# Gated feed-forward layers: high and low activation parts as one 512-column moving operand, with pairs of PSUM banks

## The reference, cut to what matters

```python
# in the first model, twice:
h = rms_norm(x, norm_ffn[l]) * (1.0 + sc_f) + sh_f
gt, up = jnp.split(h @ w_ffn_in[l], 2, axis=-1)
x = x + g_f * ((jax.nn.silu(gt) * up) @ w_ffn_out[l])
# second model, four times
def swiglu(h, w_gate, w_up, w_down):
    return (jax.nn.silu(h @ w_gate) * (h @ w_up)) @ w_down
x = x + 0.5 * swiglu(rms_norm_2(x, ffn_norm[layer, j]), ...)
```

## Time and profile before

| | |
|---|---|
| Median of 3 runs | 2282.91 us (2274.06 to 2283.78) |
| Profiled execution | 2283.06 us |
| Its span, first to last instruction | 2281.1 us |
| Mean granted TensorE clock | 0.945 of full speed |
| TensorE busy | 2092.5 us |
| VectorE busy | 1469.7 us |
| ScalarE busy | 986.5 us |

### The profile page before, as it was taken

The page is one execution under the profiler, slowest core; times in us unless marked ns, Lnnn a source line. Parts: engine busy times, 40 slices in busy tenths (PEclk is TensorE's granted clock), DMA queues, the critical chain, the costliest instruction groups (busy, mean ns, idle before and its releaser), DMA issues. The chain is left out here.

```text
span 2281.1 us, 36778 instructions
## 1 busy us (share of the span) xinstructions
PE 2092.5 (92%) x15344; PEld 1975.8 (87%) x15344; DVE 1469.7 (64%) x2515; ACT 986.5 (43%) x1486; POOL 27.5 (1%) x47
## 2 busy tenths in 40 slices
PE   3799979998799889999999888899999998789999
PEld 3678879997679879999998668799999998688999
DVE  6568667775577466547766557467657747755773
ACT  2355533333345533334335545443344335654342
POOL 0101000000001000000000000000000000000000
PEclk7789999999889989999999898999999999799999
DMA  8335537884435347555555323345555553222554
GB/s 284 128 123 187 201 103 249 272 272 141 149 134 199 112 129 231 182 179 185 184 178 193 112 74 104 119 138 182 179 186 182 181 174 114 92 93 93 185 181 134
DMA packets 266084, 372.70 MB, mean 163 GB/s; under 512 B 8384, under 2 KB 160192, under 8 KB 265920
## 3 DMA queue, kind: packets, MB, share of 16 engines
q1 hardware_dynamic: 264224, 367.48, 49.5%
q10 hardware_dynamic: 1696, 2.89, 0.3%
HBM read 369.28 MB, written 1.05 MB: 162 GB/s over the span
## 5 line engine op out<-in xcount | busy, mean ns | idle before, releaser
L2025 DVE TENSOR_TENSOR parts<-ring,parts 128x2048 fp32r<-128x2048 f32 (+4 forms) x307 | 677.8, 2209 | 489.6 <-ACT parts L653 489.2
L1337 PE MATMUL psum<-h,parts 128*128 128x256 f32 x7848 | 965.4, 285 | 27.3 <-DVE parts L2025 20.9
L1337 PEld LDWEIGHTS psum<-h,parts 128*128 128x128 f32 x7848 | 954.2, 193 | 30.2 <-issue 29.7
L653 ACT ACTIVATE parts<-ring 128x2048 fp32r<-128x2048 f32 (+3 forms) x308 | 569.5, 1849 | 869.2 <-PE psum L1337 782.7
L1337 PE MATMUL psum<-hid_hl,parts 128*128 128x256 f32 x3168 | 379.2, 282 | 1.1 <-DVE parts L2025 1.1
L1337 PEld LDWEIGHTS psum<-hid_hl,parts 128*128 128x128 f32 x3168 | 377.3, 188 | 2.0 <-issue 1.9
L1337 PE MATMUL psum<-parts,h 128*128 128x512 f32 (+1 forms) x864 | 231.1, 425 | 46.6 <-DVE parts L2025 46.6
L1337 PEld LDWEIGHTS psum<-parts,h 128*128 128x128 f32 x864 | 176.0, 214 | 87.0 <-issue 26.4
L2025 DVE TENSOR_TENSOR rot<-psum,rstd 128x256 f32<-128x256 f32 x176 | 66.6, 420 | 38.1 <-PE psum L1337 33.1
L653 ACT ACTIVATE scores_area<-scores_area,nmax 128x256 f32<-128x256 f32 (+1 forms) x160 | 72.0, 454 | 38.0 <-DVE nmax L2252 37.6
L1505 PE MATMUL psum<-feat 64*128 64x128 f32 (+4 forms) x320 | 82.6, 386 | 5.5 <-issue 4.4
(11 more groups left out here) (232 smaller groups left out, 1689.2 us busy)
## 6 DMA issues: line engine op xcount, KB each, us to landing
ring<-in_w_ada SPq DMA_DIRECT2D x48, 1024.0 KB, 5.4
ring<-in_w_ffn_in SPq DMA_DIRECT2D x88, 512.0 KB, 5.0
ring<-in_ffn_w_gate SPq DMA_DIRECT2D x88, 512.0 KB, 3.9
ring<-in_ffn_w_up SPq DMA_DIRECT2D x88, 512.0 KB, 5.0
ring<-in_w_in SPq DMA_DIRECT2D x36, 1024.0 KB, 5.1
ring<-in_ffn_w_down SPq DMA_DIRECT2D x32, 1024.0 KB, 5.1
ring<-in_w_ffn_out SPq DMA_DIRECT2D x16, 1024.0 KB, 5.0
ring<-in_ffn_w_down SPq DMA_DIRECT2D x16, 768.0 KB, 4.4
```

Of the source, the lines that this page charges most:

```text
L653: act.activation(out, in_, func, **kw).then_inc(*sig(name, *keys))
L1337: mm = pe.matmul(out, left, right, start=start and n == 0, stop=stop and n == 2, skip_group_check=True)
L2025: dve.tensor_tensor(out, a, b, op).then_inc(*sig(name, *keys))
```

## The change

In the six feed-forward layers, and in no other product, the three matmuls of a product become two (`wide_product`). The first takes the low weight by the high activation, 256 columns, into columns 0 to 255 of a bank; the second takes the high weight by both activation parts as one moving operand of 512 columns (two runs of 256), which fill the whole bank. The result of an output chunk then lies in two halves of a bank that have to be added. A job with two chunks needs two banks next to each other: `open_pair` takes the pair of (0,1), (2,3), (4,5) that was opened longest ago.

This holds for all jobs of up and for q = 0, 1 and 2 of down; q = 3 stays as it was. In all groups of up but the first, and in down, TensorE now goes through a panel job by job and no longer chunk by chunk.

ScalarE copies the second half of both banks into `low_half` (512 columns), VectorE adds it to the first halves and so frees the pair; a plain layer then multiplies the sum by rstd in a second instruction. ScalarE takes silu of the sum, VectorE multiplies, ScalarE (and no longer VectorE) makes the high part of the hidden chunk, and VectorE subtracts for the low part. Silu of job i-1 and the hidden parts of job i-2 stand behind the evacuation of job i in both programs. The first panel of the next group is split before job i = 2g, the second one before job 2g+1. `x_update` of a wide q adds the low halves of both chunks to x first, and then the high halves: four instructions for two.

The diff, with context cut down and each hunk's indentation taken away:

```diff
@@ -385,6 +385,13 @@
 piece = rot.rearrange("p a (b s) -> p (a b) s", b=2)
+low_half, both = (tok[:, 2048 + 1024 * i:3072 + 1024 * i].rearrange(
+    "p (i a s) -> p i a s", i=2, s=S) for i in range(2))
+def pair_of(job, half):
+    b = tally.bank(job)
+    return psum[:, b:b + 2, S * half:S * half + S]
@@ -1001,18 +1008,24 @@
     norm(st, ("up", f))
-for i in range(FC):
-    splits.until((("up", f), i // 2, 1), 2)
-    job = ("ffn", f, i)
-    if plain(st):
-        act.wait_ge(*at(("scaled", f, i)))
-        gate = piece[:, i % 2, :]
-    else:
-        act.wait_ge(*at(("full", job)))
-        gate = psum[:, tally.bank(job), 0:S]
+for i in range(FC + 2):
+    if i < FC:
+        splits.until((("up", f), i // 2, 1), 1 + i % 2)
+        act.wait_ge(*at(("full", ("ffn", f, i))))
+        if i >= 2:
+            act.wait_ge(*at(("sum", f, i - 2)))
+        run(low_half[:, i % 2, :, :], pair_of(("ffn", f, i), 1), ACT.Copy,
+            "act_low", ("low", f, i))
+    if 1 <= i <= FC:
+        act.wait_ge(*at(("sum", f, i - 1)))
+        if i >= 3:
+            act.wait_ge(*at(("product", f, i - 3)))
+        run(sq[:, (i - 1) % 2, 0:S], both[:, (i - 1) % 2, 0, :], ACT.Silu,
+            "act_silu", ("silu", f, i - 1))
     if i >= 2:
         act.wait_ge(*at(("product", f, i - 2)))
-    run(sq[:, i % 2, 0:S], gate, ACT.Silu, "act_silu", ("silu", f, i))
+        run(hid_hl[:, 0, i - 2, :], piece[:, (i - 2) % 4, :], ACT.Copy,
+            "act_hidden", ("hidden hi", f, i - 2))
 act.preload_act_table_set(EXP_LN)
@@ -1298,6 +1311,16 @@
+def open_pair(key):
+    first = min((0, 2, 4), key=lambda b: max(opened.get(b, -1), opened.get(b + 1, -1)))
+    for bank in (first, first + 1):
+        if bank in holder:
+            pe.wait_ge(*at(("free", holder[bank])))
+        holder[bank], opened[bank] = key, len(tally.banks)
+    tally.banks[key] = first
+    return psum[:, first:first + 2, :]
@@ -1337,6 +1360,13 @@
     return mm
+def wide_product(bank, wt_hl, act, start, stop):
+    pe.matmul(bank[:, 0:S], wt_hl[1], act[:, 0, :], start=start, stop=False,
+              skip_group_check=True)
+    return pe.matmul(bank.rearrange("p (a s) -> p a s", a=2), wt_hl[0], act,
+                     start=False, stop=stop, skip_group_check=True)
@@ -1414,9 +1444,10 @@
 def features_steps(name, g, depths, width, jobs, src, ready=None, before_last=None,
-                   pool=ROTATING, apart=False):
-    banks = [open_bank(job, pool) for job in jobs]
+                   pool=ROTATING, apart=False, wide=0):
+    banks = [open_pair(job) if j < wide else open_bank(job, pool)
+             for j, job in enumerate(jobs)]
@@ -1426,6 +1457,8 @@
 order = [(k, m) for k in range(depth) for m in range(2 * len(jobs))]
+if wide and (ready is None or name[0] == "ffnout"):
+    order.sort(key=lambda km: km[1] // 2)
@@ -1440,10 +1473,14 @@
 last = n == len(depths) - 1 and k == depth - 1
-mm = product(banks[m // 2][:, S * (m % 2):S * (m % 2) + S],
-             [a[:, k, c:c + P] for a in hl],
-             [src[:, a, k0 + k, :] for a in range(2)],
-             k0 + k == 0 and m % 2 == 0, last)
+wt = [a[:, k, c:c + P] for a in hl]
+if m // 2 < wide:
+    mm = wide_product(banks[m // 2][:, m % 2, :], wt, src[:, :, k0 + k, :],
+                      k0 + k == 0, last)
+else:
+    mm = product(banks[m // 2][:, S * (m % 2):S * (m % 2) + S], wt,
+                 [src[:, a, k0 + k, :] for a in range(2)],
+                 k0 + k == 0 and m % 2 == 0, last)
@@ -1460,7 +1497,9 @@
-features_out(st, g, depths, 512, jobs, src, ready if g == 0 else None,
+features_out(st, g, depths, 512, jobs, src,
+             wide=(2, 1)[g] if st[0] == "ffnout" else 0,
+             ready=ready if g == 0 else None, before_last=
              (lambda: early_stats(then)) if g == 1 and then is not None
@@ -1722,7 +1761,7 @@
 steps = features_steps(("up", f), i, (4, 4), 512,
-                       (lambda k: ("h", st, k)) if i == 0 else None)
+                       (lambda k: ("h", st, k)) if i == 0 else None, wide=2)
@@ -2288,11 +2327,21 @@
 dve.wait_ge(*at(("full", job)))
+wide = st[0] == "ffnout" and q < 3
+if wide:
+    settle()
+    for m in range(2):
+        c = 2 * q + m
+        stt(x[:, c, :], pair_of(job, 1)[:, m, :], gate(c), x[:, c, :],
+            ALU.mult, ALU.add)
+    settle()
 for m in range(2):
     c = 2 * q + m
     keys = [("x", st, c)] + [("free", job)] * m
-    stt(x[:, c, :], psum[:, tally.bank(job), S * m:S * m + S], gate(c),
-        x[:, c, :], ALU.mult, ALU.add, "dve_x", *keys)
+    src = (pair_of(job, 0)[:, m, :] if wide else
+           psum[:, tally.bank(job), S * m:S * m + S])
+    stt(x[:, c, :], src, gate(c), x[:, c, :], ALU.mult, ALU.add, "dve_x",
+        *keys)
@@ -2599,25 +2648,41 @@
+def gated(f, i, times=None):
+    if i < FC:
+        job, out = ("ffn", f, i), both[:, i % 2, :, :]
+        splits.until((("up", f), i // 2, 1), 1 + i % 2)
+        dve.wait_ge(*at(("low", f, i)))
+        if i >= 2:
+            dve.wait_ge(*at(("product", f, i - 2)))
+        if times is None:
+            tt(out, pair_of(job, 0), low_half[:, i % 2, :, :], ALU.add, "dve_freed",
+               ("free", job), ("sum", f, i))
+        else:
+            tt(out, pair_of(job, 0), low_half[:, i % 2, :, :], ALU.add, "dve_freed",
+               ("free", job))
+            settle()
+            tt(out, out, times, ALU.mult, "dve_step", ("sum", f, i))
+    if 1 <= i <= FC:
+        j = i - 1
+        dve.wait_ge(*at(("silu", f, j)))
+        tt(piece[:, j % 4, :], sq[:, j % 2, 0:S], both[:, j % 2, 1, :], ALU.mult,
+           "dve_step", ("product", f, j))
+    if i >= 2:
+        j = i - 2
+        dve.wait_ge(*at(("hidden hi", f, j)))
+        tt(hid_hl[:, 1, j, :], piece[:, j % 4, :], hid_hl[:, 0, j, :].bitcast(F32),
+           ALU.subtract, "dve_hidden", ("hidden", f, j))
 def ffn(f):
     pending = list(ADA_GROUPS.get(st, ()))
-    for i in range(FC):
-        splits.until((("up", f), i // 2, 1), 2)
-        job = ("ffn", f, i)
-        b = psum[:, tally.bank(job), :]
-        dve.wait_ge(*at(("silu", f, i)))
-        t = piece[:, i % 4, :]
-        tt(t, sq[:, i % 2, 0:S], b[:, S:2 * S], ALU.mult, "dve_freed",
-           ("product", f, i), ("free", job))
-        settle()
-        dve.tensor_copy(hid_hl[:, 0, i, :], t).then_inc(*sig("dve_step"))
-        settle()
-        tt(hid_hl[:, 1, i, :], t, hid_hl[:, 0, i, :].bitcast(F32), ALU.subtract,
-           "dve_hidden", ("hidden", f, i))
+    for i in range(FC + 2):
+        gated(f, i)
         if pending and i >= 6 and i % 4 == 2:
             ada_take(*pending.pop(0))
@@ -2638,31 +2703,8 @@
 refine(rstd[:], newton[:, 0, :], newton[:, 1, :])
-def finish(i):
-    t = piece[:, 2 + i % 2, :]
-    dve.wait_ge(*at(("silu", f, i)))
-    tt(t, t, sq[:, i % 2, 0:S], ALU.mult, "dve_step", ("product", f, i))
-    settle()
-    dve.tensor_copy(hid_hl[:, 0, i, :], t).then_inc(*sig("dve_step"))
-    settle()
-    tt(hid_hl[:, 1, i, :], t, hid_hl[:, 0, i, :].bitcast(F32), ALU.subtract,
-       "dve_hidden", ("hidden", f, i))
-for p in range(FC // 2):
-    splits.until((("up", f), p, 1), 1)
-    for i in (2 * p, 2 * p + 1):
-        up = ("ffn", f, i)
-        b = psum[:, tally.bank(up), :]
-        dve.wait_ge(*at(("full", up)))
-        settle()
-        tt(piece[:, i % 2, :], b[:, 0:S], rstd[:], ALU.mult, "dve_step",
-           ("scaled", f, i))
-        tt(piece[:, 2 + i % 2, :], b[:, S:2 * S], rstd[:], ALU.mult, "dve_freed",
-           ("free", up))
-    splits.until((("up", f), p, 1), 2)
-    for i in (2 * p, 2 * p + 1):
-        settle()
-        finish(i)
+for i in range(FC + 2):
+    gated(f, i, rstd[:].unsqueeze(1).broadcast_to([P, 2, S]))
 x_update(("ffnout", f), lambda c: 0.5, 6)
```

## The result

The changed kernel took **2293.43 us** (median of 6 runs, 2291.06 to 2301.85), the kernel before, run beside it, 2281.02 us (6 runs, 2274.06 to 2283.78). The ratio is 1.0062 with a 95% interval of 1.0041 to 1.0084: slower by about 12 us, where 2282 and "no change" were forecast. The time itself lies at the upper end of the forecast case's own range (2272 to 2294). The profiled execution took 2295.05 us, its span is 2293.2; that of before took 2283.06 with a span of 2281.1.

A forecast was written before the change was run, and what follows sets the result against it. The prediction took the six feed-forward layers to run at TensorE's own pace. Its terms, -36.6 + 6.8 + 9.9 + 11.4 + 7.4 = -1.1 us, gave 2282 us, with an 8-in-10 range of 2256 to 2306.

The forecast's parts named there:

- forecast case: Whole kernel: product 346.7 ns in up, 345.4 in down, waits nearly cancel the gain; 2282 us, chance 0.52.
- The pace: Up and down: one matmul fewer saves 13.3 ns a product in up, 10.7 in down; 36.6 us gained.
- steps 1 to 4: TensorE waits: ahead of group 1 6.8 us, down's third panel 9.9, down's second half 11.4, layer ends 7.4.
- The delay after a cross stage: Start of the layer following a cross stage: q = 2's bank delays it by 0.35 us each.
- Late pairs in every group: Group openings: add 0.5 us later than planned costs each of 60 openings 0.4 us; +24, 2306 us; chance 0.20.
- Load hidden: Up and down: weight load hides behind the 512-column stream, product 328 ns; 2252 us; chance 0.12.
- Edge waits absent: Waits ahead of down's third panel and second half do not come, 21 us stay; 2261 us; chance 0.12.
- Saving not there: Up and down: matmul overhead goes with the columns, product stays at 360 ns; 2315 us; chance 0.04.

The follow-up runs named there:

- Experiment 5: Changed kernel with the matmul of 512 columns split into two of 256, pairs, evacuation and order kept: 2319.26 us, ratio 1.0171 to the kernel before.
- Experiments 1: Changed kernel with q = 2 of down back to three narrow matmuls and a single bank: 2277.01 us, ratio 0.9992 to the kernel before.
- 10: Changed kernel with down's q = 2 narrow, group 0's second panel job-sorted, down's third-panel hi early in layers 1 to 5, warm-up before layers 3 and 5: 2262.45 us.
- 3: Changed kernel with the second panel of group 0 sorted by job as well: 2285.41 us, ratio 1.0017 to the kernel before.
- 4: Changed kernel with the high part of down's third panel made ahead of the table load: 2293.85 us, ratio 1.0056 to the kernel before.

## Why the prediction was wrong

**"The pace", the price of a product: mis-sized, the larger part of the miss.** I carried the 13.3 ns that each of two uniform rows pays over to a row that alternates. In the fast rhythm of up this holds, 347 ns against 346.7 forecast; but layers 2 and 5 ran at 353 and layer 4 did for half of its groups, which no row of before shows, and down ran at 351 instead of 345.4. With the measured means up gains (360.0 - 349.9) x 2112 = 21.3 us and down (356.1 - 351.1) x 792 = 4.0: **25.3 us in place of 36.6**. Experiment 5 gives about the same from whole runs: 26, with two more stretches at half clock in it and some waits that the slower TensorE hides. My range for the product, 342 to 351, just held the mean of each, but not layers 2 and 5. Its upper end was the safer case, given that the short row of 512 columns already showed 236 ns and not 226.7.

The Trainium skill (page TensorE: Matmul & The Clock Gate, section Back-to-back issue gap) gives N/2.4 + 2.5 ns for a matmul, 325 ns for this pair as an estimate. It gives this as the gap of a single matmul on its own, without a weight load, which the prediction left out when it took it as a rule for these rows. Every rhythm here is at least 22 ns above it.

**What follows a wait: a missing term.** I costed each wait at its own length and had TensorE go on at full clock. After an idle of 2.2 us it ran a part of the first panel at half clock, 1.5 us lost each time; five times makes 7.5 us in the profiled execution. Experiments 1 and 10 show it from two sides: idle away, half clock away; idle filled, half clock away. Not every such idle has it (see the last section), so that five came in this execution, and not three or seven, is chance as far as the runs show.

**The waits, steps 1 to 4: right in the main.** All four came at the places named, for the reasons named, with the sizes given in the section on the result. The delay after a cross stage was 0.77 us (1.42 to 2.19 in layer 3) and not 0.35. And down's third panel cost 1.7 instead of 2.0, since the table load began 7.3 us after the end of up instead of 7.6 and TensorE, at the slower pace, came 0.2 later. Experiments 1, 3 and 4 each removed the waits whose reason they removed. In the sum they were to cost 35.5 us. With them and the two corrections, for the profiled execution, the sum is -25.3 + 35.5 + 7.5 = +17.7, and the profiled executions differ by 12.0. The other 5.7 us: 3.7 of them lie ahead of the change. Layer 0, the first layer that it touches, starts at 335.41 us, and in the execution of before at 339.07; over the kernels here, which are the same up to there, it starts anywhere from 333.0 to 340.7. Another 2.2 are down's third panel, 7.6 us in all layers (1.7 in each plain one, 0.9 in layer 1, none in layer 0) where 9.9 were forecast. The plan for the layers thus held to within the noise once pace and clock are put right. Between the starts of layers 3 and 4 nothing of that kind interferes: the layer went from 192.52 us (1501.25 to 1693.77) to 195.56 (1499.67 to 1695.23), and each stretch can be read by itself.

| Layer 3 | Before, us | After, us | Difference |
|---|---|---|---|
| Start to group 1 | 13.72 | 16.09 | +2.37: wait, 1.5 of clock, less 0.4 of pace |
| Group 1 to down | 115.20 | 111.09 | -4.11: pace alone |
| Down to its third panel | 11.39 | 12.89 | +1.50: wait |
| Third panel to second half | 20.31 | 21.96 | +1.65: wait |
| Second half to layer 4 | 31.90 | 33.53 | +1.63: wait |

**The rivals.** Late pairs in every group: not there, with one late group in six layers. Load hidden: the product would be 328. Edge waits absent: they are all there. Saving not there (2315, given 0.04): wrong too as a whole, but it was the only one that doubted the price of the wide matmul, and a third of the saving was indeed not there. The miss is of the forecast case itself: its two errors, 11 and 7 us, went the same way. The chance for "slower" should have come from the forecast's own upper tail, for which I left 0.02. Within the profiled execution some luck went the other way: layer 3 had the fast rhythm throughout, and the layers began 3.7 us early.

## What to carry to other kernels

A saving per instruction that runs through thousands of copies is best priced from a row with the same alternation; without one, take the slower of the paces that the rows allow, because the whole gain is that small difference. A wait that a change puts in front of a long busy stretch can cost its length and then the clock: here 2.2 us of idle came, most of the times, with another 1.5. And where a change has a bulk part that gains and edges that lose, cost it part by part: here up alone was even with the kernel before (0.9989, interval 0.9972 to 1.0007), down with its two groups only lost, and three small moves at the edges made a slower kernel one that is faster than before by 0.7%, and by 0.9% with the warm-up.

## What the runs showed of the hardware that I had not expected

- **Two rhythms for the same row.** Alternating matmuls of 256 and 512 columns, each with its own load, run at 347 ns a product (117 + 230) or at 353, in a cycle of three products whose starts are 113 + 233, 117 + 241 and 120 + 236 ns apart. There is no wait and no change of the clock between the two; the same layer can have the other in the next kernel. Over the ten profiled kernels with the wide operand, that is 40 plain layers, 17 are in the slow rhythm from group 1 on, 3 are in the fast one to the end, and 20 change once, from fast to slow. None changes back. In layers 0 and 1, where ada_cols stand between groups, it goes both ways. What makes it fall into the slow one is open. The starts of matmuls in layer 2, which is in the slow one, against layer 3:

```profile
1060.50 0.28 PE L1366 MATMUL psum<-h,parts 128*128 128x256 f32 x1
1060.62 0.40 PE L1368 MATMUL psum<-h,parts 128*128 128x512 f32 x1
...
1061.56 0.28 PE L1366 MATMUL psum<-h,parts 128*128 128x256 f32 x1
1061.68 0.40 PE L1368 MATMUL psum<-h,parts 128*128 128x512 f32 x1
```

```profile
1530.42 0.28 PE L1366 MATMUL psum<-h,parts 128*128 128x256 f32 x1
1530.54 0.39 PE L1368 MATMUL psum<-h,parts 128*128 128x512 f32 x1
...
1531.46 0.28 PE L1366 MATMUL psum<-h,parts 128*128 128x256 f32 x1
1531.58 0.39 PE L1368 MATMUL psum<-h,parts 128*128 128x512 f32 x1
```

Three products take 1.06 us in the first and 1.04 in the second. Six ns in 2112 products are 12.7 us, so this may be a good part of the spread of these kernels' times (2276.93 to 2296.91 in experiment 3); no run tied a single time to its rhythm.
- **A short wait can cost clock.** In layers 2 to 5 of the changed kernel the clock stayed at 2.4 GHz after the idles ahead of group 1 and of down's third panel and fell to 1.2 GHz after those at the starts. The equally long one ahead of down's second half brought the half level in layer 4 and not in layer 3, and in experiment 4 layer 4 started at full clock after 2.1 us. Over all eleven kernels with pairs, layers 2 to 5: of 28 starts after an unfilled idle of 2.1 to 2.4 us, 24 were followed by a stretch at half clock; of 24 second halves of down after an idle of 2.0 to 2.1 us, 11; of 28 third panels after 1.3 to 1.5 us, none. So the length of the wait alone does not decide it. What else does is open.
